# The gates' products of a streaming encoder step: from split passes on the whole array to full precision in four column groups

## What is computed

```python
def project(xn, w_in, b_i, b_f, q_norm_g, k_norm_g):
    aq, ak, av, mq, mk, mv, mi, mf, mo = split_in(xn @ w_in)
    ...
    ig = mi.astype(f32) + b_i.astype(f32)
    lf = jax.nn.log_sigmoid(mf.astype(f32) + b_f.astype(f32))
```

## Time and profile before

| | |
|---|---|
| median of 3 runs | 1754.9 us (1754.14 to 1755.54) |
| the profiled execution | 1757.45 us |
| its span, first to last instruction | 1755.6 us |
| TensorE (PE) busy | 1744.9 us, 99% |
| VectorE (DVE) busy | 898.7 us, 51% |
| ScalarE (ACT) busy | 669.1 us, 38% |
| GpSimd (POOL) busy | 207.1 us, 12% |
| mean granted TensorE clock | 1.000 |

### The profile page before, as it was taken

How to read it: one execution, slowest core, us unless ns; L and a number is a source line. 1 busy time by engine, 2 the same in 40 slices (tenths; PEclk the granted TensorE clock), 3 DMA queues, 4 the chain that set the end, 5 groups by cost and what they waited for, 6 DMA issues and landing times.

```text
span 1755.6 us, 27160 instructions
## 1 busy us (share of the span) xinstructions
PE 1744.9 (99%) x9270; PEld 1582.7 (90%) x9270; DVE 898.7 (51%) x1718; ACT 669.1 (38%) x1256; POOL 207.1 (12%) x286
## 2 busy tenths in 40 slices
PE   9999999999999999999999999999999999999999
PEld 7999998899997789999888999888999888999887
DVE  5634776666677645454344454344444334545333
ACT  5323754444354444333332333333333333333332
POOL 3301010002352210110000110000111000111000
PEclk9999999999999999999999999999999999999999
DMA  7675469998798554444344444334443434444442
GB/s 182 189 181 149 122 163 222 197 202 217 198 258 261 152 142 115 125 121 130 121 131 120 128 122 123 129 124 127 121 130 120 131 120 130 121 122 129 141 147 96
DMA packets 381393, 261.54 MB, mean 149 GB/s; under 512 B 92444, under 2 KB 328156, under 8 KB 381324
## 3 DMA queue, kind: packets, MB, share of 16 engines
q1 hardware_dynamic: 353190, 222.09, 45.1%
q0 software_dynamic: 13072, 34.68, 7.6%
q10 hardware_dynamic: 15062, 3.86, 1.1%
HBM read 244.90 MB, written 21.46 MB: 152 GB/s over the span
## 4 chain that ended last, share of the span: by engine, by line
PE 96%; DVE 2%; SPq 1%; DMA 1%; issue 0%; ACT 0%; ACTq 0%; DVEq 0%
PE acc L520 18%; PE acc L521 18%; PE acc L522 17%; PE bank L607 8%; PE bank L608 8%; PE bank L606 8%; PE bank L1895 3%; PE ssb L606 2%; PE ssb L607 2%; PE ssb L608 2%; PE ssb L1895 1%; PE bank L566 1%; PE bank L567 1%; PE bank L565 1%; SPq L874 1%; PE acc L565 1%
## 5 line engine op out<-in xcount | busy, mean ns | idle before, releaser
L500 DVE TENSOR_TENSOR w_lo<-raw,w_hi 128x512 fp32r<-128x512 f32 x768 | 556.6, 733 | 780.5 <-ACT w_hi L491 779.9
L491 ACT ACTIVATE w_hi<-raw 128x512 fp32r<-128x512 f32 x768 | 482.2, 630 | 830.4 <-PE acc L522 402.6
L521 PE MATMUL acc<-x2g_lo,w_hi 128*128 128x384 f32 x1024 | 348.0, 340 | 0.0
L520 PE MATMUL acc<-x2g_hi,w_hi 128*128 128x384 f32 x1024 | 345.8, 338 | 0.0
L522 PE MATMUL acc<-x2g_hi,w_lo 128*128 128x384 f32 x1024 | 344.6, 337 | 0.0
L520 PE MATMUL acc<-a_hi,w_hi 128*128 128x400 f32 (+1 forms) x768 | 268.1, 349 | 0.2 <-DVE w_lo L500 0.2
L521 PE MATMUL acc<-a_lo,w_hi 128*128 128x400 f32 (+1 forms) x768 | 262.9, 342 | 0.0
L522 PE MATMUL acc<-a_hi,w_lo 128*128 128x400 f32 (+1 forms) x768 | 262.3, 342 | 0.0
L607 PE MATMUL bank<-w_lo,a_hi 128*128 128x512 f32 x640 | 253.0, 395 | 0.0
L608 PE MATMUL bank<-w_hi,a_lo 128*128 128x512 f32 x640 | 252.6, 395 | 0.0
L606 PE MATMUL bank<-w_hi,a_hi 128*128 128x512 f32 x640 | 252.0, 394 | 0.0
(11 more groups left out here) (339 smaller groups left out, 1517.0 us busy)
## 6 DMA issues: line engine op xcount, KB each, us to landing
raw<-in_w_up SPq DMA_DIRECT2D x128, 512.0 KB, 4.0
raw<-in_w_down SPq DMA_DIRECT2D x128, 512.0 KB, 3.7
raw<-in_w_in SPq DMA_DIRECT2D x94, 512.0 KB, 4.6
raw<-in_w_out SPq DMA_DIRECT2D x32, 512.0 KB, 4.6
vc<-in_cache_v POOLq DMA_DIRECT2D x32, 256.0 KB, 6.8
kc<-in_cache_k SPq DMA_DIRECT2D x128, 64.0 KB, 3.1
state_blocks<-in_state_C POOLq DMA_DIRECT2D x16, 256.0 KB, 4.5
C_blk<-state_blocks SPq DMA_DIRECT2D x4, 1024.0 KB, 8.9
```

What stands on the lines that cost most here:

```text
L491: e.activation(w_hi[:, q], raw[:, slot, 4 * (q % 2):4 * (q % 2) + 4, :], ACT.Copy).then_inc(hi_ready, 1)
L500: e.tensor_tensor(w_lo[:, q], raw[:, slot, 4 * (q % 2):4 * (q % 2) + 4, :], w_hi[:, q].bitcast(F32), ALU.subtract).then_inc(lo_ready, 1)
L520: e.matmul(out, w_hi[:, q, kk], hi[:, k, at], start=k == 0, stop=False, skip_group_check=True)
L521: e.matmul(out, w_hi[:, q, kk], lo[:, k, at], start=False, stop=False, skip_group_check=True)
```

## The change

The input is joined again: GpSimd adds `a_hi` and `a_lo` into 16 blocks of full fp32, twelve in `zt` (its tiles 4 to 15, not yet in use) and four in `m1`. The gate weights are loaded straight into `gw`, 32 columns to a feature block, and are not split. Each feature block is one product in full fp32, with 32 output rows, and four blocks in a row go to the four column groups of the array, whose results land in rows 0, 32, 64 and 96 of the bank. VectorE scales the four parts by `rstd_x` and adds them, two parts in `gate(0)`, two in `gate(1)`.

```diff
-GATE_W, GATE_LO = 64, 32
+GATE_W = 32
+X_IN_ZT = 12
...
+        def x_full(k):
+            return zt[:, KT - X_IN_ZT + k] if k < X_IN_ZT else m1[:, k - X_IN_ZT]
...
+            def join_x(ks):
+                for k in ks:
+                    read_out(e, ("xT", k))
+                    e.tensor_tensor(x_full(k), a_hi[:, k].bitcast(F32), a_lo[:, k].bitcast(F32),
+                                    ALU.add).then_inc(S("x_joined"), 1)
+
+            join_x(X_AHEAD)
             e.wait_ge(S("x_in3"), 16 * X_PIECES[3])
+            e.wait_ge(S("gw_padded"), 1)
...
-                dma(gw_raw[:],
+                dma(gw[:, :, 0:2 * NH],
                     w_in[0, :, N_GATE:N_MO].rearrange("(k p) n -> p k n", p=P), "gw_in")
+                join_x(range(X_AHEAD.stop, KT))
                 dma(g2[:], norm2_g[0].rearrange("(k p) -> p k", p=P), "params")
...
-                if r == 1:
-                    e.wait_ge(S("gw_in"), 16)
-                    e.wait_ge(S("gw_padded"), 1)
-                    e.activation(gw_hi, gw_raw[:], ACT.Copy).then_inc(S("gw_hi_made"), 1)
...
-            def gates_lo(q):
-                if q == 2:
-                    e.wait_ge(S("gw_hi_made"), 1)
-                    tt(gw_lo, gw_raw[:], gw_hi.bitcast(F32), ALU.subtract).then_inc(S("gw_lo_made"), 1)
...
+            def gate_part(b, g, to):
+                rows = slice(GATE_W * g, GATE_W * g + 2 * NH)
+                return tt(to[0:2 * NH], b[rows, 0:TOK], rstd_x[rows], ALU.mult)
+
             def gate(n):
                 if n == 0:
                     b = take(e, "gates")
-                    low = slice(GATE_LO, GATE_LO + 2 * NH)
-                    step(tt(lf[0:2 * NH], b[low, 0:TOK], rstd_x[low], ALU.mult))
-                    step(tt(gate8[0:2 * NH], b[0:2 * NH, 0:TOK], rstd_x[0:2 * NH], ALU.mult))
-                    taken(tt(gate8[0:2 * NH], gate8[0:2 * NH], lf[0:2 * NH], ALU.add), "gates")
-                    read_out(e, "gates")
+                    gate_part(b, 0, gate8)
+                    step(gate_part(b, 1, lf))
+                    step(tt(gate8[0:2 * NH], gate8[0:2 * NH], lf[0:2 * NH], ALU.add))
                     e.wait_ge(S("params"), 16 * 20)
                 elif n == 1:
+                    b = take(e, "gates")
+                    gate_part(b, 2, bcum)
+                    step(gate_part(b, 3, mrow))
+                    step(tt(bcum[0:2 * NH], bcum[0:2 * NH], mrow[0:2 * NH], ALU.add))
+                    taken(tt(gate8[0:2 * NH], gate8[0:2 * NH], bcum[0:2 * NH], ALU.add), "gates")
+                    read_out(e, "gates")
                     step(ts(ipre[0:NH], gate8[0:NH], gate_b[:, 0:1], None, ALU.add))
...
-            e.wait_ge(S("gw_lo_made"), 1)
+            e.wait_ge(S("gw_in"), 16)
             gates = fill(e, "gates")
             for k in range(KT):
-                w = gw[:, GATE_W * k:GATE_W * k + P]
-                mm(gates[:, 0:TOK], w, a_hi[:, k], k == 0, False)
-                last = mm(gates[:, 0:TOK], w, a_lo[:, k], False, k == KT - 1)
+                g = k % 4
+                if g == 0:
+                    e.wait_ge(S("x_joined"), k + 4)
+                last = mm(gates[GATE_W * g:GATE_W * (g + 1), 0:TOK], gw[:, k], x_full(k), k < 4, k >= KT - 4)
```

More of the change, by code:

```diff
@@ L358, in build @@
             diag = sb("diag", [P, 4, P], scope=s)
-            gw_raw = sb("gw_raw", [P, KT, 8], scope=s)
-            gw = sb("gw", [P, (KT + 1) * GATE_W], F32R, scope=s)
-            gw_hi, gw_lo = (gw[:, 0:KT * GATE_W].rearrange("p (k n) -> p k n", n=GATE_W)[:, :, at:at + 8] for at in (0, GATE_LO))
+            gw = sb("gw", [P, KT, GATE_W], scope=s)
             rb_b = sb("rb_b", [NH * BUCKETS, P], scope=s)
@@ L650, in _ @@
             dma(xn[0:TAIL, 3, later], x_prompt[0, 2 * P - META:SEQ, later], "x_small")
-            e.memset(gw[:].bitcast(F32), 0.0).then_inc(S("gw_padded"), 1)
+            e.memset(gw[:], 0.0).then_inc(S("gw_padded"), 1)
             e.tensor_copy(ones_r[:], ones[:]).then_inc(S("ones_r_made"), 1)
+            def join_x(ks):
[4 more added lines that the diff above has]
+            join_x(X_AHEAD)
             e.wait_ge(S("x_in3"), 16 * X_PIECES[3])
+            e.wait_ge(S("gw_padded"), 1)
             with nc.allow_non_contiguous_dma("small parameters, one element per partition"):
-                dma(gw_raw[:],
+                dma(gw[:, :, 0:2 * NH],
                     w_in[0, :, N_GATE:N_MO].rearrange("(k p) n -> p k n", p=P), "gw_in")
+                join_x(range(X_AHEAD.stop, KT))
                 dma(g2[:], norm2_g[0].rearrange("(k p) -> p k", p=P), "params")
@@ L958, in square_rows @@
                 e.wait_ge(S("x_squared"), r + 1)
-            def rows_and_gates(r):
-                square_rows(r)
-                if r == 1:
-                    e.wait_ge(S("gw_in"), 16)
-                    e.wait_ge(S("gw_padded"), 1)
-                    e.activation(gw_hi, gw_raw[:], ACT.Copy).then_inc(S("gw_hi_made"), 1)
-            split_hi(e, 0, 1, after=rows_and_gates)
+            split_hi(e, 0, 1, after=square_rows)
             e.wait_ge(S("x_mean"), 1)
@@ L1260, in _ @@
             split_lo(e, 0, 0, after=lambda q: x_lo(X_LATER[q]))
-            def gates_lo(q):
-                if q == 2:
-                    e.wait_ge(S("gw_hi_made"), 1)
-                    tt(gw_lo, gw_raw[:], gw_hi.bitcast(F32), ALU.subtract).then_inc(S("gw_lo_made"), 1)
-            split_lo(e, 0, 1, after=gates_lo)
+            split_lo(e, 0, 1)
             e.wait_ge(S("x_squared"), 4)
```

## The result

The changed kernel took 1761.58 us (median of 6, 1759.67 to 1763.25), the kernel before 1754.31 in the same rounds: a ratio of 1.0042, 95% interval 1.0032 to 1.0051, or +7.3 us. The prediction had +3.0, and its range ended at 1760.9. The profiled execution took 1763.25 us.

A forecast was written before the change was run, and what follows sets the result against it. TensorE, busy 1744.9 of 1755.6 us, was taken as the bound. Terms -2.8 (gates), +0.3 (tile 2's `w_lo`), +0.4 (held `w_lo`), +5.1 (`lamp`) gave +3.0 on the median 1754.9: 1757.9 us, range 1754.2 to 1760.9.

The forecast's parts named there:

- the one on holding: GpSimd's joins beside VectorE's `w_lo`: each `w_lo` gets in between two joins, six delay the joins by 3.7 us to 36.0.
- The term of 0.4: Tile 0's last quarter: its `w_lo` comes at most one join later, 0 to 1 us, taken as +0.4 us.
- The late parameters: VectorE's wait behind the first gate step: parameters land at 49.8, VectorE stands some 4 us, TensorE about 5 at `lamp`.
- my rival's 32.3: GpSimd is not held: joins end at 32.3, parameters land at 46.1, -0.7 us, 1754.2; chance 0.13.
- the forecast's chain: Joins end at 36.0, parameters land at 49.8, TensorE goes on at `lamp` at 53.6 after a wait of about 5 us.
- The clock: Rival: the clock falls in TensorE's 5 us gap at `lamp`, adding 1.6 us (1 to 3): +4.6, 1759.5; chance 0.33.
- my two main cases: Parameters late, joins held: clock stays, 1757.9 us, chance 0.42; or the same with a fallen clock, 1759.5, chance 0.33.
- the gates at a quarter of the array's time: Gate products on four overlapping column groups: 8 take 1.56 us, 16 take 3.1, freeing 2.8 us.
- 0.3 for tile 2's `w_lo`: Behind the gates TensorE is ready 2.4 us after `rstd` starts, `w_lo` at 2.7: a wait of 0.3 us.
- no price for the splits and the fill: Dropping two gate-weight splits on ScalarE and VectorE and shortening GpSimd's zero fill of `gw` changes nothing.
- the cap: If parameters are not late, four extra gate operations hold `lamp` to about 49.4, capping the gain at 1.2 us; chance 0.04.
- twelve: In the kernel before, the last parameter lands at 33.5, said to be twelve us early.

The follow-up runs named there:

- joins alone: The kernel before plus the same 16 joins on GpSimd, results unused, TensorE waiting for them ahead of the gates: 1763.52 us, 1.0054.
- no joins: The changed kernel without the 16 joins; the gates read `a_hi` alone, leaving out the input's low part: 1753.29 us, 0.9996.
- fills: The kernel before with seven zero fills of 128x1088 on GpSimd in the joins' place, about 1 us each: 1754.13 us, 1.0001.
- the wait behind each join: The changed kernel, with GpSimd waiting after each join for that join's own semaphore: 1758.85 us, 1.0028.
- one join queued: The changed kernel, with GpSimd waiting behind join k for join k-1, so one join is queued behind the running one: 1763.76 us, 1.0057.

## Why the prediction was wrong

**The step that failed** is the one on holding: "with joins standing back to back, a `w_lo` gets in only between two of them", and from it, `w_lo` "comes at most one join later: 0 to 1 us, taken as 0.4". I had one example of a hold, in which GpSimd ran a single operation, and I read a run of twelve as twelve such examples with a gap behind each. There was no gap. The term of 0.4 measured 8.4 us (tile 0 to the gates, 29.35 against 20.93). That it was the joins is shown (joins alone, no joins), and that a GpSimd busy with fills does not do it; that one queued join can be enough, too; why VectorE got in at times, at 11.63 in the changed kernel's own trace among others, stays open.

**The late parameters** were the consequence of the same error. If VectorE cannot get in, GpSimd is not held: the joins ended at 31.5, which was my rival's 32.3. That rival had -0.7 us, because it gave GpSimd the way and charged VectorE nothing for it. One of the two must pay, and here it was VectorE, on whose `w_lo` TensorE waits. With the wait behind each join the forecast's chain came true in its place, and nearly in its size: the joins ended at 34.9 (forecast 36.0), `lamp` came at 52.46 (53.6), behind a wait of 3.7 us (5.1).

**The clock** did fall in a gap, but in tile 0, and its price depended on what was next: nothing in front of another hold, 1.7 us where TensorE was the bound. My 1.6 is near that, in part by luck: it came from eight products' records at the start, and not from what stands behind a gap in the middle. The measured total fits neither of my two main cases; the nearer one, +4.6 with a fallen clock, had its terms at other places.

**Right:** the gates at a quarter of the array's time (1.48 us for half of them, forecast 1.56); 0.3 for tile 2's `w_lo` (measured 0.47); no price for the splits and the fill; and the cap, which said that the four new operations hold `lamp` once nothing else does and leave 1.2 us of the gain: without the joins 2.2 - 1.3 = 0.9 us are left by the trace, 0.7 by the medians. One reading was off without effect: the parameters before landed 14 us ahead of VectorE's wait for them (33.5 against 47.7), not twelve.

## What to carry to other kernels

Work that is given to an idle engine is not free if it reads where a critical engine reads: look at what the neighbour's instructions of that moment read, and price the whole run of the new instructions, not one. A single hold in a trace gives the price of one instruction, not that of a row without a break; here a wait behind each instruction turned it back into single holds. And where two engines share something, a rival in which neither pays is not a rival.

## What was not expected of the hardware

GpSimd operations that read two tensors of SBUF and start 0.98 us apart kept a VectorE operation with two SBUF inputs out for seven of them (7.49, 7.55 and 7.44 us in three kernels) and for nine in another; zero fills of the same length did not, and `a_lo`, from a bank, was not held. Others of the same `w_lo`, beside the same joins, were held by one join only (1.12 us at 11.63, 1.61 with one join queued). A fall of the granted clock behind 5.3 us without work lasted 9 us of time (two stretches of 12 products, 0.32 apart) in one execution; behind 5.4 us, in another kernel, it was over by the third quarter. The length of the wait did not settle whether it fell: it did behind 1.65 us in one kernel, and did not behind the 2.1 us of the earlier trace rows.
